# Feed forward: rows' high and low part in one matmul of 512 columns, halves summed on VectorE, modulation's sums in the fourth bank

## What is computed

```python
D_FF = 2816
def swiglu(h, w_gate, w_up, w_down):
    return (jax.nn.silu(h @ w_gate) * (h @ w_up)) @ w_down

def first_block(...):
    for l in range(2):
        ...
        h = rms_norm(x, pre_ffn_g[l])
        x = x + rms_norm(swiglu(h, w_gate[l], w_up[l], w_down[l]), post_ffn_g[l])
```

## Time and profile before

| | us |
|---|---|
| median of 3 runs | 2267.62 (2267.57 to 2268.7) |
| the profiled execution | 2265.01 |
| its span | 2263.2 |
| layer 0, round 0 to the last down | 263.0 to 456.4 |
| layer 1, the same | 685 to 878 |
| experts | from about 1000 |

### The profile page before, as it was taken

The page is one execution under the profiler, slowest core; times in us unless marked ns, Lnnn a source line. Parts: engine busy times, 40 slices in busy tenths (PEclk is TensorE's granted clock), DMA queues, the critical chain, the costliest instruction groups (busy, mean ns, idle before and its releaser), DMA issues.

```text
span 2263.2 us, 28736 instructions
## 1 busy us (share of the span) xinstructions
PE 1796.1 (79%) x12614; PEld 1155.1 (51%) x12614; DVE 814.9 (36%) x1237; ACT 529.5 (23%) x797; POOL 88.2 (4%) x136
## 2 busy tenths in 40 slices
PE   8999999999999999998665666666666666666566
PEld 7898999999889998864211111211112111121111
DVE  5755677767567776851100100101010010010101
ACT  5745534356444334630000000000000000000000
POOL 1200000012100000000000000000000000000000
PEclk9999999999999999999878878887887887887887
DMA  8445667754545775499999999999999999999997
GB/s 267 132 162 177 196 224 238 238 161 158 188 155 199 252 248 178 186 392 429 430 428 429 428 429 429 429 429 430 428 429 429 428 429 430 429 429 429 429 429 316
DMA packets 172077, 739.80 MB, mean 327 GB/s; under 512 B 6784, under 2 KB 133248, under 8 KB 146992
## 3 DMA queue, kind: packets, MB, share of 16 engines
q1 hardware_dynamic: 169600, 731.27, 81.3%
q0 software_dynamic: 2352, 6.69, 0.8%
HBM read 736.88 MB, written 1.05 MB: 326 GB/s over the span
## 4 chain that ended last, share of the span: by engine, by line
DMA 49%; PE 42%; DVE 5%; ACT 3%; issue 1%; POOL 0%; SPq 0%; DVEq 0%; POOLq 0%; ACTq 0%
PE PS L369 41%; DMA WB<-in_w_down 24%; DMA WB<-in_w_up 24%; DVE WL L1706 1%; ACT WH L1162 1%; DVE S L1701 1%; DVE X L1701 1%; DMA W<-in_w_gate 0%; POOL T L2546 0%; PE PS L468 0%; DMA W<-in_w_in 0%; DVE S L1698 0%; DVE CN L1698 0%; ACT HTh L1223 0%; PE PS L597 0%
## 5 line engine op out<-in xcount | busy, mean ns | idle before, releaser
L369 PE MATMUL PS<-WB,XS 128*32 128x352 f32 x3360 | 397.5, 634 | 242.4 <-DMA WB<-in_w_up 165.4
L369 PEld LDWEIGHTS PS<-WB,XS 128*32 128x32 f32 x3360 | 125.8, 140 | 509.3 <-DMA WB<-in_w_up 221.0
L1706 DVE TENSOR_TENSOR WL<-W,WH 128x2048 fp32r<-128x2048 f32 x138 | 317.0, 2297 | 135.2 <-ACT WH L1162 135.0
L1701 DVE SCALAR_TENSOR_TENSOR S<-S,PS 128x352 f32<-128x352 f32 (+1 forms) x110 | 63.3, 587 | 749.5 <-PE PS L369 427.8
L369 PE MATMUL PS<-WB,S 128*32 128x512 f32 (+1 forms) x1204 | 229.9, 722 | 120.5 <-DMA WB<-in_w_down 94.6
L369 PE MATMUL PS<-HTh,WH 128*128 128x256 f32 x1064 | 307.3, 289 | 7.9 <-DVE HTl L1701 5.4
L1162 ACT ACTIVATE WH<-W 128x2048 fp32r<-128x2048 f32 x141 | 269.5, 1911 | 183.0 <-PE PS L369 178.0
L369 PE MATMUL PS<-HTl,WH 128*128 128x256 f32 x1064 | 301.5, 283 | 0.0
L369 PE MATMUL PS<-HTh,WL 128*128 128x256 f32 x1064 | 301.4, 283 | 0.0
L369 PEld LDWEIGHTS PS<-HTh,WH 128*128 128x128 f32 x1064 | 204.3, 192 | 12.6 <-DVE WL L1706 5.4
L369 PEld LDWEIGHTS PS<-HTl,WH 128*128 128x128 f32 x1064 | 204.5, 192 | 0.9
(11 more groups left out here) (283 smaller groups left out, 2159.5 us busy)
## 6 DMA issues: line engine op xcount, KB each, us to landing
WB<-in_w_up SPq DMA_DIRECT2D x63, 2816.0 KB, 36.4
WB<-in_w_gate SPq DMA_DIRECT2D x47, 2816.0 KB, 35.6
WB<-in_w_down SPq DMA_DIRECT2D x46, 2816.0 KB, 36.1
CN<-in_w_gate SPq DMA_DIRECT2D x16, 2816.0 KB, 36.7
CN<-in_w_down SPq DMA_DIRECT2D x16, 2816.0 KB, 36.6
W<-in_w_in SPq DMA_DIRECT2D x31, 1024.0 KB, 5.4
S<-in_w_ada SPq DMA_DIRECT2D x24, 1024.0 KB, 5.5
W<-in_w_gate SPq DMA_DIRECT2D x22, 1024.0 KB, 7.9
```

The source lines that it names most:

```text
L369: return e.matmul(o, l, r, start=start, stop=stop, skip_group_check=True)
L1701: return e.scalar_tensor_tensor(out=o, in0=a, scalar=s, in1=b, op0=o1, op1=o2)
L1706: e.tensor_tensor(M.WL[i][:, :], M.SLOT[m % NW], M.WH[i][:, :].bitcast(F32), ALU.subtract).then_inc(*up("low", m))
```

## The change

`HTh` and `HTl` become one tensor, `HT2` [128, 2, 8, 256]. In gate and up `proj_t` gives way to `proj_halves`: each half j of the output columns has a bank of its own, and for each chunk k there is one matmul of 512 columns, `WH` by both parts of the rows, whose results lie side by side in the bank, and one of 256, `WL` by the high part, added to the first half. So the bank holds two halves that must be summed. ACT copies the second halves of both banks to `FG` (gate) or `FU` (up) in SBUF, DVE adds the first halves to them, 256 values in each of two instructions, and tanh and the products read `FG` and `FU`. Gate has banks 0 and 1 of the four, up 2 and 3; modulation's sums go into the fourth bank, between gate and up. Both products on DVE stand behind `WL` of gate n+1, where before the first stood ahead of it. The hidden values' product now signals `f_prod`.

```diff
+    def proj_halves(name, l, n, to, b, norm=None):
+        m, u = unit(name, l, "cols", n)
+        for j in range(2):
+            ps = given((*to, j), b + j)
+            for k in range(8):
...
+                w = part(u, slice(None), k, slice(128 * j, 128 * j + 128))
+                mm(two(ps), w[0], M.HT2[:, :, k, :], k == 0, False)
+                ins = mm(ps[:, 0:256], w[1], HT[0][:, k, :], False, k == 7)
...
-        ps, acc, ones = take(("ada", n)), products(i, M), M.CST[:, C_ONES:C_ONES + 128]
+        ps, acc, ones = given(("ada", n), 3), products(i, M), M.CST[:, C_ONES:C_ONES + 128]
...
-            proj_t("w_gate", l, n, HT, ("g", l, n), norm=("ffn", l) if n == 0 else None)
+            proj_halves("w_gate", l, n, ("g", l, n), 0, ("ffn", l) if n == 0 else None)
             ada_sum(12 * l + n)
-            proj_t("w_up", l, n, HT, ("u", l, n))
+            proj_halves("w_up", l, n, ("u", l, n), 2)
...
+        def halves(o, what, l, n, b):
+            full(what, l, n, 1)
+            if n:
+                e.wait_ge(*at("f_prod", l, n - 1))
+            e.activation(o, PS[:, 4 + b:6 + b, 256:512], ACT.Copy).then_inc(*up("f_half", what, l, n))
...
-            stt(flat(A), flat(A), 1.0, g, ALU.add, ALU.mult).then_inc(*freed("g", l, n))
+            def halves(o, what):
+                e.wait_ge(*at("f_half", what, l, n))
+                for j in range(2):
+                    e.tensor_tensor(o[:, j, :], full(what, l, n, j)[:, 0:256], o[:, j, :], ALU.add).then_inc(*freed(what, l, n, j))
+            halves(M.FG, "g")
             next(job)
...
-            stt(flat(A), flat(A), 0.5, u, ALU.mult, ALU.mult).then_inc(*freed("u", l, n))
+            e.wait_ge(*at("f_tanh", l, n))
+            stt(flat(A), flat(A), 1.0, flat(M.FG), ALU.add, ALU.mult).then_inc(*step())
+            halves(M.FU, "u")
+            own()
+            for j in range(2):
+                e.wait_ge(*free("u", l, n, j))
+            stt(flat(A), flat(A), 0.5, flat(M.FU), ALU.mult, ALU.mult).then_inc(*up("f_prod", l, n))
```

More of the change, by code:

```diff
@@ L258, in memory @@
         M.MEM = [sb(n, [128, 8, 256], F32R, first) for n in ("MEMh", "MEMl")]
-        M.HT = [sb(n, [128, 8, 256], F32R, first) for n in ("HTh", "HTl")]
+        M.HT2 = sb("HT", [128, 2, 8, 256], F32R, first)
+        M.HT = [M.HT2[:, i] for i in range(2)]
         M.W = sb("W", [128, 2048 * NW], F32, first)
@@ L319, in memory @@
     M.A = [view(512 * i, 2, 256) for i in range(2)]
+    M.FG, M.FU = view(1024, 2, 256), view(1536, 2, 256)
     M.AK = view(2048, 8, 128)
@@ L360, in take, with given @@
         return PS[:, 4 + i, :]
+    def given(name, i):
+        i, k = C.banks.give(name, i)
+        if k > 1:
+            e.wait_ge(C.sig.sem(f"bank{i}"), k - 1)
+        return PS[:, 4 + i, :]
     def free(*use):
@@ L397, in proj_t @@
         same(("full", *to), ("unit", m))
+    def proj_halves(name, l, n, to, b, norm=None):
[3 more added lines that the diff above has]
+            for k in range(8):
+                if norm and j == 0:
+                    e.wait_ge(*at("lo", norm, k))
+                w = part(u, slice(None), k, slice(128 * j, 128 * j + 128))
+                mm(two(ps), w[0], M.HT2[:, :, k, :], k == 0, False)
+                ins = mm(ps[:, 0:256], w[1], HT[0][:, k, :], False, k == 7)
+            if j:
+                ins.then_inc(*up("unit", m))
+            beside.step()
+        for j in range(2):
+            same(("full", *to, j), ("unit", m))
     def proj_r(name, l, n, src, to, off=0):
@@ L1493, in ffn @@
             unit()
[L1494 to L1497, removed]
+            halves(M.FG, "g", l, n, 0)
             if n > 1:
@@ L1501, in ffn @@
                 early()
-            e.wait_ge(*free("u", l, n))
+            if n >= 2:
+                e.wait_ge(*at("hid", l, n - 2))
+            for j in range(2):
+                e.wait_ge(*free("g", l, n, j))
+            e.activation(flat(A), flat(M.FG), ACT.Tanh, scale=0.5).then_inc(*up("f_tanh", l, n))
+            halves(M.FU, "u", l, n, 2)
+            e.wait_ge(*at("f_prod", l, n))
             if n < 4:
@@ L2209, in ffn @@
             next(job)
-            g, u = flat(two(full("g", l, n))), flat(two(full("u", l, n)))
-            e.wait_ge(*at("f_tanh", l, n))
-            stt(flat(A), flat(A), 1.0, g, ALU.add, ALU.mult).then_inc(*freed("g", l, n))
+            def halves(o, what):
+                e.wait_ge(*at("f_half", what, l, n))
+                for j in range(2):
+                    e.tensor_tensor(o[:, j, :], full(what, l, n, j)[:, 0:256], o[:, j, :], ALU.add).then_inc(*freed(what, l, n, j))
+            halves(M.FG, "g")
             next(job)
@@ L2218, in ffn @@
                 early()
-            e.wait_ge(*free("g", l, n))
-            stt(flat(A), flat(A), 0.5, u, ALU.mult, ALU.mult).then_inc(*freed("u", l, n))
+            e.wait_ge(*at("f_tanh", l, n))
+            stt(flat(A), flat(A), 1.0, flat(M.FG), ALU.add, ALU.mult).then_inc(*step())
+            halves(M.FU, "u")
+            own()
+            for j in range(2):
+                e.wait_ge(*free("u", l, n, j))
+            stt(flat(A), flat(A), 0.5, flat(M.FU), ALU.mult, ALU.mult).then_inc(*up("f_prod", l, n))
             e.wait_ge(*at("f_hi", l, n))
```

## The result

The changed kernel has a median of 2289.2 us (2286.7 to 2290.5, 4 runs) against 2267.6: a ratio of 1.0094, 95% interval 1.0081 to 1.0106. It is slower, as forecast, but by 21.6 us and not by 13.5, and lies above the range. Its profiled execution took 2286.74 us with a span of 2284.9, 21.7 more than before.

The account below looks back on a forecast made before the run. It took TensorE as bounding the dense rounds, with VectorE's loop close behind. Layer 0's +6.5 and layer 1's +7.0 gave +13.5 us: 2265.0 becomes 2278.5 profiled, median 2281, range 2274 to 2288.

Parts of the forecast that it names:

- the loop: Chain from `WH` of gate n+1 through `WL`, product, `MXh` and up's weights to up n+1's end; slack 0.7 normally.
- The first rival: TensorE's gain comes through: 44 x 0.20 less long-loop limits, 2259.6 us, faster; chance 0.05.
- the banks: Waits for gate's and up's banks: harmless from round 3 on; gate 2 of layer 0 waits for gate 1's, +0.5.
- round 0's gain: Layer 0's feed forward: T of round 0 comes 0.20 us earlier.
- the mixed stream: Gate and up's alternating 512- and 256-column matmuls: 5.56 us a unit instead of 5.76, bounds 5.16 and 5.76.
- the 1.40: Time in us added on VectorE before the hidden values' product: first product 0.60, up's additions 0.34 and 0.46.
- short-loop round: Normal round with a modulation sum and a 0.91 us quarter in the loop: 17.41 becomes 17.93, +0.52.
- long-loop one: Round with a quarter half as long again and no modulation sum: 17.20 becomes 18.40 us, +1.20.
- layer 0's last down: It waits for a modulation sum of 1.8 us anyway, which hides its late `WL`: no loss.
- layer 1's first three rounds: Long quarters and a late gate 3 load: T moves from 740.07 to 742.2, +2.1 us.
- the pair's and the addition's bounds: Pair: 0.40 a loop below, 0.20 above; addition: 0.15, each over 16 loops; sum 5 to 19 us.
- The fourth rival: Loads come late: SP's weight loads queue behind a modulation load awaiting VectorE's sums; 2290 us, chance 0.10.

Follow-up runs that it names:

- e5_first: As e1_bank, but VectorE's first product ahead of `WL` of gate n+1 and tanh ahead of its `WH` on ScalarE; 2277.01 us (1.0044).
- e4_late: Kernel before, matmuls and banks untouched, with the changed kernel's VectorE order and two additions nobody reads before the hidden values' product; 2283.23 us (1.0059).
- e1_bank: Changed kernel with banks of gate and up swapped in layer 0 alone, modulation's sums in bank 1; 2284.66 us (1.0067).
- e3_nosums: As e1_bank, but second halves computed and never added; ScalarE and VectorE work as in the kernel before; 2267.47 us (0.9993).

## Why the prediction was right in kind and wrong in size

**The bound.** Right. The rounds were TensorE's with a loop close behind, the loop closed at the places named, and e5_first, e4_late and e1_bank show that its length sets the round with 0.87, 1.38 and 1.49 us added to it (17.53, 18.08 and 18.13 us, e4_late's with the old, longer up). The first rival, TensorE's gain coming through, fell with them.

**The first step that failed: the banks.** The prediction checked bank waits "from round 3 on", and worked out those of rounds 0 to 2, but only against the round before. It didn't ask who had bank 0 before gate 0 came, and it took round 0's gain (T 0.20 earlier) as certain. A copy of 0.65 us on ScalarE, queued behind the eight that make the rows' high part, held it; 3.5 us with the clock's fall, shown by e1_bank. The diff says it in one word, `given` in place of `take`.

**The second: the mixed stream.** Predicted 0.2275 + 0.12 a chunk and 5.56 a unit. In the changed kernel, rounds 3 to 10 of layer 0, a merged matmul stands 0.2356 from its successor and the one of 256 columns 0.1171: 0.3527, and 5.64 a unit. So merging saves 0.007 a chunk there, and 0.010 in e3_nosums (0.2341 + 0.1157), not 0.0125. The forecast's value was the best of its rows but lay off. The Trainium skill's 2.5 ns ("TensorE: Matmul & The Clock Gate", section "Wait — 56ns, not 53.3ns?"), by which a pair saves 0.0025, lies off on the other side of the 0.007 to 0.010 measured. All in all 44 x 0.11 to 0.16 = 5 to 7 us was the most that TensorE could give, not 8.8. In a loop-bound round it counts once, since only up's length is in the loop: 5.64 against 5.56, +0.08.

**The third: the 1.40.** The product started at T + 5.07 before (counted from gate 0 they stand behind up 4, not up 3, which changes nothing in the sum) and starts at 347.81, T + 6.56, now: 1.49. The additions came as predicted (0.75 for two, overlapped, against 0.34 + 0.42), but behind them VectorE needed 0.14 and not 0.04 until the product. That product waits for three semaphores in a row; e4_late's waits for two, and starts 0.03 after its additions. That the waits make the difference is likely but not shown. +0.09 a loop. With the second term it makes 18.1 and 18.6 where I had 17.93 and 18.40: some 0.17 over 16 loops, 2.7 us.

**Terms that held**, but for these 0.17 a loop: +0.52 for a short-loop round (0.71), +1.20 for a long-loop one (1.38), rounds 0 to 2 of layer 0 without gate 0 +0.3 (0.4), nothing at layer 0's last down, +1.1 at layer 1's (1.2), layer 1's first three rounds +2.1 (2.3), the experts' stage unchanged.

**The sum again**: 13.5 + 3.5 + 2.7 = 19.7, where the trace has 20.2 without the 1.5 us of the start. The medians differ by 21.6. The remaining 1.4 to 1.9 us stay open: e1_bank's median is 4.5 below the changed kernel's, its trace only 3.5 (and the start's scatter) better, and the changed kernel's four runs lie 3.8 us apart.

**The range** took the pair's and the addition's bounds, and had no room for a term that the sum didn't hold. The fourth rival would have covered the size, 2290, but by a mechanism that wasn't there.

## What to carry to other kernels

Where TensorE is at 9 tenths, close the loops of the other engines with their durations before believing its digits: a round of matmuls that gets shorter only shows what was second, and work added to an engine with 30% of idle time costs its length, once the loop's slack (0.7 us here in a normal round) is used up, if it stands between a wait and the instruction that the next round's weights hang on. When a change takes buffers out of rotation, go to the last user of each before the first round and not only around the loop. And when work is moved later in a queue, look at every load that waits for its result, and at all loads behind that one.

## What was unexpected of the hardware

Around a wait of 3.0 us the granted clock was 0.66 over 5 us, and the eight matmuls after it ran at the 1.2 GHz level, for 2.7 us; with a wait of 0.52 at the same place (e1_bank) it stayed at 1.00. So 2.5 us of additional waiting cost 3.5. The pattern of one matmul of 512 columns and one of 256, with two weight tensors in turn, ran at 0.350 to 0.353 us for 768 columns, and not at 0.2275 + 0.12 = 0.3475 as the rows of either length alone would have it; where the moving columns lie has no part in that, and what has stays open.
